# Four input sums on GpSimd, three constant products and a later start of the last weight copies in a float32 kernel for two blocks of layers

## The reference

```python
o = from_blocks(o).reshape(b, s, INNER)
y = (o * jax.nn.silu(g)) @ w_out           # g: a quarter of x @ w_in
x = layer_norm(ALPHA * x + y, ln_g[i], ln_b[i])

def layer_norm(x, g, b):
    mu = jnp.mean(x, axis=-1, keepdims=True)
    var = jnp.mean(jnp.square(x - mu), axis=-1, keepdims=True)
    return (x - mu) * lax.rsqrt(var + LN_EPS) * g + b
```

## Time and profile before

| | |
|---|---|
| three timed runs | 1541.19, 1541.31, 1543.64 us; median 1541.31 |
| the profiled execution | 1542.46 us, of which 1540.5 are its span |
| TensorE busy | 1515.3 us (98%), mean granted clock 0.998 |
| VectorE, ScalarE, GpSimd busy | 1152.0, 887.0, 768.8 us |

### The profile page before, as it was taken

How to read it: one execution, slowest core, us unless ns; L and a number is a source line. 1 busy time by engine, 2 the same in 40 slices (tenths; PEclk the granted TensorE clock), 3 DMA queues, 4 the chain that set the end, 5 groups by cost and what they waited for, 6 DMA issues and landing times.

```text
span 1540.5 us, 21821 instructions
## 1 busy us (share of the span) xinstructions
PE 1515.3 (98%) x7792; PEld 1293.6 (84%) x7792; DVE 1152.0 (75%) x2064; ACT 887.0 (58%) x1544; POOL 768.8 (50%) x726
## 2 busy tenths in 40 slices
PE   9999999999999999999999999999999999999997
PEld 7888899988888888888888888887888988888877
DVE  5999999998664687437717559967777828988977
ACT  6445788787433344324324464689995327777753
POOL 2232345435465477557747563456655424444443
PEclk9999999999999999999999999999999999999999
DMA  7889765665332222323222278856457945456551
GB/s 222 194 186 203 165 137 130 146 161 126 123 107 91 91 96 96 110 83 110 96 96 89 96 180 188 177 130 140 110 126 177 202 106 132 109 123 137 109 121 59
DMA packets 60299, 203.26 MB, mean 132 GB/s; under 512 B 6816, under 2 KB 9376, under 8 KB 60192
## 3 DMA queue, kind: packets, MB, share of 16 engines
q0 software_dynamic: 19008, 69.21, 26.3%
q1 hardware_dynamic: 40896, 132.14, 25.8%
q10 hardware_dynamic: 288, 0.52, 0.1%
HBM read 199.75 MB, written 2.10 MB: 131 GB/s over the span
## 4 chain that ended last, share of the span: by engine, by line
PE 84%; DVE 7%; ACT 5%; DMA 2%; issue 1%; POOL 1%; DVEq 0%; SPq 0%; POOLq 0%; ACTq 0%
PE bank L368 82%; PE bank L374 2%; DVE r L407 1%; DMA w_raw<-in_weights 1%; ACT k_both L378 1%; ACT prob L378 1%; ACT w_hi L378 1%; DVE pt_lo L395 1%; DMA w_lo<-in_weights 1%; DVE prob L1288 0%; ACT pt_hi L378 0%; DVE r L395 0%; DVE q_both L407 0%; DVE score L1875 0%; ACT soft L378 0%
## 5 line engine op out<-in xcount | busy, mean ns | idle before, releaser
L414 POOL TENSOR_TENSOR w_lo<-w_raw,w_hi 128x512 fp32r<-128x512 f32 (+1 forms) x190 | 278.5, 1485 | 210.3 <-ACT w_hi L378 210.3
L378 ACT ACTIVATE w_hi<-w_raw 128x1024 fp32r<-128x1024 f32 (+2 forms) x206 | 213.9, 1041 | 278.7 <-PE bank L368 253.3
L368 PE MATMUL bank<-x_hi,w_hi 128*128 128x512 f32 x872 | 346.6, 398 | 1.3 <-DVE k_lo_first L407 0.6
L368 PE MATMUL bank<-x_hi,w_lo 128*128 128x512 f32 x872 | 340.6, 391 | 0.6 <-DMA w_lo<-in_weights 0.4
L368 PE MATMUL bank<-x_lo,w_hi 128*128 128x512 f32 x872 | 340.1, 390 | 0.0
L368 PEld LDWEIGHTS bank<-x_hi,w_lo 128*128 128x128 f32 x872 | 163.7, 188 | 37.0 <-POOL w_lo L414 0.8
L368 PEld LDWEIGHTS bank<-x_hi,w_hi 128*128 128x128 f32 x872 | 163.9, 188 | 33.4 <-ACT k_both L378 1.0
L368 PEld LDWEIGHTS bank<-x_lo,w_hi 128*128 128x128 f32 x872 | 164.2, 188 | 29.8
L621 POOL DMA_DIRECT2D w_lo<-in_weights x132 | 117.0, 894 | 120.4 <-ACT w_lo L378 96.3
L368 PE MATMUL bank<-a_hi,w_hi 128*128 128x512 f32 x416 | 162.0, 389 | 0.0
L368 PE MATMUL bank<-a_hi,w_lo 128*128 128x512 f32 x416 | 161.8, 389 | 0.0
(11 more groups left out here) (230 smaller groups left out, 3403.5 us busy)
## 6 DMA issues: line engine op xcount, KB each, us to landing
w_raw<-in_weights SPq DMA_DIRECT2D x223, 512.0 KB, 3.4
w_lo<-in_weights POOLq DMA_DIRECT2D x132, 512.0 KB, 6.6
alibi<-in_alibi SPq DMA_DIRECT2D x16, 256.0 KB, 3.9
w_raw<-in_weights SPq DMA_DIRECT2D x8, 384.0 KB, 3.0
r<-in_x SPq DMA_DIRECT2D x8, 256.0 KB, 6.1
r<-in_x SPq DMA_DIRECT2D x4, 512.0 KB, 6.2
out_y<-r SPq DMA_DIRECT2D x16, 128.0 KB, 1.8
w_raw<-in_weights ACTq DMA_DIRECT2D x2, 256.0 KB, 4.2
```

The lines of the kernel that those rows point to most:

```text
L368: return e.matmul(out, lhsT, rhs, start=start, stop=stop, skip_group_check=resumed)
L378: return self.act.run(lambda e: e.activation(out, in_, func, **kw), after, 0.07 + size(out) * 0.00086 + 0.09 * len(kw))
L414: return self.pool.run(lambda e: e.tensor_tensor(out, a, b, op), after, cost)
```

## The change

The change has four parts.

- `slot_ready` has chunks of out_b in the slots 5 and 6 wait also for `os_ready` of the last pair, that is for its high and low parts. These are the chunks 231 and 232.
- `sum_x`, started in `project_and_norm` of the last layer, adds `x_hi` and `x_lo` of the tiles 4 to 7 on GpSimd in place of `x_hi`, at due times 1.4 apart, once the last product that reads the input is done. `mix_evict` waits for that sum and uses it in one VectorE instruction instead of two.
- `half_norm` puts three constant products ahead of the sum over tile 7 in the second half.
- The pace of the first half's finishing steps goes from 1.5 to 1.2.

```diff
@@ -249,6 +249,7 @@
             self.w_lo.append(at(f"w_lo{LOWS + i}", a + 4, [CHUNK], F32R))
         self.x_hi = at("x_hi", 44, [KT, S], F32R)
         self.x_lo = at("x_lo", 60, [KT, S], F32R)
+        self.x_sums = at("x_sums", 44, [KT, S])
         self.r0 = at("r0", 76, [KT, S])
         self.r0v = at("r0v", 76, [PAIRS, NT, P])
         self.r1 = at("r1", 92, [KT, S])
@@ -558,8 +559,10 @@
 
         after = [(yield from self.know(self.chunk_in, c))]
         if self.slots[c] >= 3:
-            scores, weights = yield from self.know(self.phase_done, more_slots(self.plan[c])[0])
+            scores, weights, outputs = yield from self.know(self.phase_done, more_slots(self.plan[c])[0])
             after += yield from self.know(scores if self.slots[c] in AFTER_SCORES else weights, HEADS - 1)
+            if self.plan[c][0] == "out_b" and self.slots[c] in AFTER_WEIGHTS:
+                after += yield from self.know(outputs, PAIRS - 1)
         if before is not None:
             after.append((yield from self.know(self.chunk_done, before)))
         return after
@@ -1482,10 +1485,10 @@
 
     def reset_heads(self, name):
         self.qk_ready, self.s_done, self.t_done, self.pv_done = {}, {}, {}, {}
-        self.phase_done[name] = (self.s_done, self.pv_done)
         self.half_ready = {}
         self.bias_used, self.p_ready, self.v_split, self.o_ready, self.half_free = {}, {}, {}, {}, {}
         self.exps, self.pt_ready, self.os_ready = {}, {}, {}
+        self.phase_done[name] = (self.s_done, self.pv_done, self.os_ready)
 
     def heads(self, v_all, *amounts):
 
@@ -1957,6 +1960,15 @@
 
     def begin_norm(self):
         self.u_ready, self.u_sum, self.u_sq = {}, {}, {}
+        self.x_sum, self.x_summed = {}, ()
+
+    def sum_x(self, used):
+
+        for c in self.x_summed:
+            hi, lo = self.x_hi[:, c, :].bitcast(F32), self.x_lo[:, c, :].bitcast(F32)
+            yield [used]
+            self.x_sum[c] = [self.p_tt(self.x_sums[:, c, :], hi, lo, ALU.add, [used])]
+            yield 1.4
 
     def mix_evict(self, key, b, t, halves=(0, 1)):
 
@@ -1966,10 +1978,12 @@
         cols = slice(HALF * halves[0], HALF * halves[0] + n)
         su, sq, acc = self.ext[0][:, cols], self.ext[1][:, cols], self.ext[2][:, cols]
         u = self.r0[:, c, cols]
-        t = self.v_stt(u, self.x_hi[:, c, cols].bitcast(F32), 2.0 * ALPHA, b.ap[:, 0:n], ALU.mult, ALU.add,
-                       [t] + self.v_split[PAIRS - 1])
+        summed = (yield from self.know(self.x_sum, c)) if c in self.x_summed else []
+        x = self.x_sums[:, c, cols] if summed else self.x_hi[:, c, cols].bitcast(F32)
+        t = self.v_stt(u, x, 2.0 * ALPHA, b.ap[:, 0:n], ALU.mult, ALU.add, [t] + self.v_split[PAIRS - 1] + summed)
         b.release([t])
-        t = self.v_stt(u, self.x_lo[:, c, cols].bitcast(F32), 2.0 * ALPHA, u, ALU.mult, ALU.add, [t])
+        if not summed:
+            t = self.v_stt(u, self.x_lo[:, c, cols].bitcast(F32), 2.0 * ALPHA, u, ALU.mult, ALU.add, [t])
         for half in halves:
             u_ready[(c, half)] = t
         yield [t]
@@ -1997,6 +2011,9 @@
         self.ring = self.psum
         for half in range(2):
             self.start(self.half_norm(half, self.u_ready, self.u_sum, self.u_sq, *norm))
+        if self.last_norm:
+            self.x_summed = range(FIRST_HALVED[name], KT)
+            self.start(self.sum_x(self.chunk_done[self.plan.index(("gb", PAIRS - 1))]))
         hi, lo = (lambda k: self.o_hi[:, k, :]), (lambda k: self.o_lo[:, k, :])
         os_ready = self.os_ready
         first = FIRST_HALVED[name]
@@ -2018,6 +2035,8 @@
         self.column_sums(b, NT, self.ext[2], False, False, [t_q], tiles)
         t_u = yield from self.know(u_sum, end)
         t_q = yield from self.know(u_sq, end)
+        if half and self.last_norm:
+            yield from self.keep_busy(3)
         yield [t_u]
         self.column_sums(b, 0, self.r0[:, KT - 1, :], False, False, [t_u], tiles)
         yield [t_q]
@@ -2326,7 +2345,7 @@
         self.project_and_norm("out_a", 3, "ln_g0", "ln_b0", self.next_x, (2.0, 1.5))
         self.stick_mixer()
         self.last_norm = True
-        self.project_and_norm("out_b", 4, "ln_g1", "ln_b1", self.result, (1.5, 0.4))
+        self.project_and_norm("out_b", 4, "ln_g1", "ln_b1", self.result, (1.2, 0.4))
         self.settle()
         self.sp.wait(self.stored)
```

## The result

| | before | changed |
|---|---|---|
| median of 21 runs | 1543.37 us | 1546.87 us |
| lowest and highest | 1541.18 to 1547.05 | 1544.07 to 1548.85 |
| ratio | | 1.0023, 95% interval 1.0016 to 1.0029 |
| the profiled execution's span | 1540.5 us | 1542.8 us |

The change makes the kernel slower, by some 3.5 us. Both kernels scatter by about 5 to 6 us from run to run, and the first three runs of before, on which the forecast stood, were on the low side. In the changed kernel the time goes with the mean granted clock of the execution: five runs with 0.997 took 1544.07 to 1545.77 us, six with 0.995 took 1547.04 to 1548.85. The profiled one (1544.7 us) is one of the five, so it is quicker than most.

What follows compares the result with a forecast made beforehand. TensorE, busy for 98% of the span, was taken to bound the kernel. The terms -0.23 + 0 + 0 + 0.4 - 0.8 = -0.6 us took 1541.31 to 1540.7 us, with a range of 1538.9 to 1542.6.

Steps and rivals of the forecast that it cites:

- Part 1: Last weight copies behind the last low part: TensorE's wait at 1498 us goes, gain 0.23 us; low weights in time, cost 0.
- Part 2: First half, tiles 4 to 7: GpSimd's additions leave VectorE 0.7 us behind, slack absorbs it: 0, bounds -0.2 and +1.4 us.
- rival A: First half: GpSimd's additions lock VectorE out, tile 4 is 4.1 us late, TensorE waits 1.4 us: 1542.1 us; chance 0.12.
- the rule of the Trainium skill: Shared SBUF port: a two-SBUF-input VectorE instruction behind a GpSimd instruction reading SBUF is blocked until that one ends.
- Part 3: Second half's last sums: three more products start the sum over tile 7 later, cost 0.4 us, bounds -0.45 and +0.7.
- no slow clock is there for them to mend: Second half's last sums: granted clock is 1.00 at 1529 to 1532 us, so the three products have nothing to mend.
- Part 4: Tail: the shorter pace takes two VectorE multiplications out, VectorE ends last there, gain 0.80 us, bounds 0 and -1.4.
- B: First half, tiles 6 and 7: low weights land too late, TensorE waits 1.4 to 2.8 us: 1542.1 to 1543.5; chance 0.15.
- C: Last sums and tail: the products find a gap and the tail gives more, -2.1 us, 1539.2 us; chance 0.13.
- D: Tail: the pace does nothing, moved steps cost ahead of the statistics what they save: +0.2, 1541.5 us; chance 0.12.

Runs made afterwards that it cites:

- e5: The kernel before with only the later start of the last two chunks' copies: median 1543.80 us, ratio 1.0000 against before.
- e3: The changed kernel with the four GpSimd additions moved ahead of the copies of chunks 231 and 232: median 1542.79 us, ratio 1.0002 against before.
- e8: The changed kernel with four constant products ahead of the first half's sums, where TensorE waits: median 1544.98 us, ratio 1.0009 against before.
- e1: The changed kernel without the four GpSimd additions, tiles 4 to 7 again evicted in two VectorE instructions: median 1543.28 us, ratio 1.0001 against before.
- e12: The changed kernel with two GpSimd additions (tiles 6 and 7) instead of four: median 1544.08 us, ratio 1.0008 against before.
- e4: The changed kernel without the three constant products ahead of the last sums: median 1546.95 us, ratio 1.0026 against before.
- e2: The kernel before with the four GpSimd additions alone: median 1548.24 us, ratio 1.0038 against before.
- e6: The kernel before with only the pace of 1.2 instead of 1.5: median 1543.83 us, ratio 1.0001 against before.
- e10: The changed kernel with additions early, without the three products, the second half's eight sums behind tile 7's last product: median 1542.38 us, ratio 0.9991 against before.

## Why the prediction was wrong, point by point

**Part 1** was right: 0.69 us for the low part, no wait of TensorE, copies four in a row, issues at 1499.49 with a median of 6.3 us to landing, no wait for a low weight. By e5 it is worth nothing that can be measured; 0.23 us are below what the medians can tell.

**Part 2, "the slack takes it up: 0"**, is the step that failed, twice. First the size of VectorE's delay. I took one stretched instruction (0.69 to 1.29 us) beside a single GpSimd addition and multiplied it by four. When both engines have such instructions back to back, three of VectorE's four take 1.78 and GpSimd's 1.75 each: 3.5 us more on VectorE instead of 2.4. The last sum of squares, 0.44 us ahead of TensorE before, is 1.3 us later in the stretch (it ends at 1515.65), and TensorE waits 1.0 us, 0.36 of it because the planner also moved the sums three products forward. That is rival A in kind: VectorE comes 3.5 us late to tile 4 where A had 4.1, and the wait is 1.0 where A had 1.4. On the rule of the Trainium skill weighed there (SBUF — State Buffer, "Who interferes with whom"): in this run the two engines go in step, one instruction of each per 1.71 us (1504.66 to 1511.52 for four), less than the 1.98 of one after the other (1.29 and 0.69; by the distances of 1.25 and 0.61 at which each follows its like alone in e3 it would be 1.86); so the trace agrees that they block each other, and not that the second waits for the whole of the first. Second, a term that the sum lacked: a wait of TensorE costs more than its length where the clock falls behind it. e8 shows it by filling the wait. It is 1.5 us here, and none of my cases had it; hence a range that ended 4.3 us below the measured median, of which some 2 us are that the three runs shown for before were lower than the 21.

**Part 3** had the sign and size of the total (0.4 later to the sum over tile 7), and that is luck: it came about in another way. The working was right for the order that it took as given; e1 and e12 keep the eight sums behind tile 7's last product, and there u's sum starts 1.59 us behind the eight instead of 1.14, 0.45 later. In the changed kernel the products cost nothing (e4). What costs is that the eight sums moved ahead of tile 7's last products, out of the wait that they filled: with VectorE relieved of one instruction a tile, their due time in the planner came earlier (e2, the additions alone, has the new order; e1, all but the additions, the old one). And "no slow clock is there for them to mend" was wrong for the changed kernel: without them it is there (e4, e2).

**Part 4** was wrong: not 0.8 us gained but nothing (e6). The tail's last VectorE addition waits for ScalarE's eighth shift, which ends 3.75 us behind the first; I counted VectorE's work there and didn't ask what it waits for. And only one multiplication left the tail, not two; with two gone (e10) it is as long.

**The sum**, read off the stretch: 1.0 (wait) + 1.5 (clock) + 0.4 (order of the eight sums), with 0.1 for the first half's eight sums, which take longer, = 3.0 of 3.07 us. Rivals B, C and D did not occur, save for D's result.

## What to carry to other kernels

Additions moved to an idle GpSimd are paid by VectorE if both read two inputs from SBUF at the same time; put them where VectorE is idle (e3), and price them by rows in which both engines are busy back to back. A wait of TensorE beside small products is to be priced with the clock behind it. And where a planner orders a queue by due times, relieving one engine moves others' instructions, forward into waits (the first half's sums) and out of waits that they filled (the second half's).

## What the runs showed of the hardware that I had not expected

- Beside some 1.8 us of products with one column, one wait of 0.86 to 0.89 us (by the row; the changed kernel, e4) and one of 0.35 with one of 0.52 (e2) were followed by 3.5 and 7 us at a granted clock of 0.54, and one of 0.51 (e12) by 3.5 us at 0.62. The same products without a wait were not (before, e1, e3, e10), nor with the wait filled (e8). At the second half's sums 0.51 us of wait did it (e2, e4), and 0.18 and 0.27 (e6) didn't.
- GpSimd additions and VectorE additions of 128x512 from SBUF, both back to back, take 1.75 and 1.78 us instead of 1.28 (e3) and 0.69. A VectorE instruction of that size with one input in a PSUM bank isn't stretched: that of 1503.25 in the changed kernel took 0.68 us beside GpSimd's addition of 1503.41.
